# Latent attention: heads one at a time, the next pair's projections cut into pieces and set between the items, values multiplied so that the output comes out by feature

## The reference, cut to what matters

```python
q = jnp.einsum("bsc,chd->bshd", c_q, w_uq)              # 128 + 64 features for each head
q_nope, q_rope = q[..., :QK_NOPE], apply_rope(q[..., QK_NOPE:], cos, sin)
k_nope = jnp.einsum("bsc,chd->bshd", c_kv, w_uk)
v = jnp.einsum("bsc,chd->bshd", c_kv, w_uv)
s = (q_nope . k_nope + q_rope . k_rope) * scale         # causal mask, k_rope shared by the heads
p = softmax(s)
o = einsum("bhqk,bkhd->bqhd", p, v)
y = o.reshape(bsz, seq, N_HEADS * V_DIM) * silu(gate)
return y @ w_out
```

## Time and profile before

| what | value |
|---|---|
| median of three runs | 2797.47 us (2796.53 to 2798.96) |
| the profiled execution: time / span of its core | 2798.33 us / 2796.3 us |
| mean granted TensorE clock | 0.980 of full speed |
| busy over the span: PE, DVE, ACT, POOL | 2657.9, 1300.7, 719.2, 879.8 us |
| latent attention core, first projection to `wob` | 2320.0 to 2682.0 us |
| busy in it: PE, DVE, ACT | 322.6, 210.4, 85.1 of 362.0 us |

### The profile page before, as it was taken

One profiled execution on the slowest core, in us unless ns is written; L12 is line 12 of the kernel. 1 busy time (PEld: TensorE's weight loads), 2 busy tenths in 40 slices (PEclk: granted clock), 3 DMA queues, 4 the chain that ended last, 5 costly groups with the idle time before them and its releaser, 6 DMA issues. The chain is left out here.

```text
span 2796.3 us, 33364 instructions
## 1 busy us (share of the span) xinstructions
PE 2657.9 (95%) x13072; PEld 2194.7 (78%) x13072; DVE 1300.7 (47%) x1648; ACT 719.2 (26%) x941; POOL 879.8 (31%) x660
## 2 busy tenths in 40 slices
PE   6999999899899999999999999999998999898986
PEld 5888887677688888888888878788786778788875
DVE  4475533466453322123212464577845225555543
ACT  5144244222221200000000123455524122212221
POOL 3454423111233333333333443333343222110111
PEclk9999999999999999999999999999999999999998
DMA  3100121101341111111111112211133110000021
GB/s 125 46 31 31 42 72 38 53 35 46 147 143 46 49 49 47 51 45 53 45 53 46 68 53 83 87 45 45 45 127 112 42 56 29 19 10 15 23 83 68
DMA packets 44499, 160.72 MB, mean 57 GB/s; under 512 B 4720, under 2 KB 9072, under 8 KB 41968
## 3 DMA queue, kind: packets, MB, share of 16 engines
q1 hardware_dynamic: 38336, 124.53, 13.1%
q10 hardware_dynamic: 6064, 34.78, 3.3%
HBM read 138.33 MB, written 20.97 MB: 57 GB/s over the span
## 5 line engine op out<-in xcount | busy, mean ns | idle before, releaser
L428 POOL TENSOR_TENSOR derived_vectors<-w_staged 1x1 f32<-1x1 f32 x208 | 51.1, 246 | 1820.5 <-PE ps L544 1308.4
L431 POOL TENSOR_TENSOR w_low<-w_staged,w_high 128x1024 fp32r<-128x1024 f32 x208 | 557.3, 2679 | 16.7
L542 PE MATMUL ps<-h_ffn_high,w_high 128*128 128x512 f32 x832 | 324.6, 390 | 1.6 <-DVE ple_proj L1778 1.6
L544 PE MATMUL ps<-h_ffn_high,w_low 128*128 128x512 f32 x832 | 323.7, 389 | 0.0
L543 PE MATMUL ps<-h_ffn_low,w_high 128*128 128x512 f32 x832 | 323.7, 389 | 0.0
L607 PE MATMUL ps<-h_mix_high,w_high 128*128 128x512 f32 x688 | 281.9, 410 | 0.0
L609 PE MATMUL ps<-h_mix_high,w_low 128*128 128x512 f32 x688 | 269.2, 391 | 0.0
L608 PE MATMUL ps<-h_mix_low,w_high 128*128 128x512 f32 x688 | 268.1, 390 | 0.0
L429 POOL CAST w_high<-w_staged 128x1024 fp32r<-128x1024 f32 x208 | 215.0, 1034 | 0.0
L1760 DVE TENSOR_TENSOR squares<-ps,rstd 128x512 f32<-128x512 f32 x88 | 60.5, 689 | 322.1 <-PE ps L544 311.7
L542 PEld LDWEIGHTS ps<-h_ffn_high,w_high 128*128 128x128 f32 x832 | 156.2, 188 | 34.9 <-issue 2.5
(11 more groups left out here) (344 smaller groups left out, 5388.1 us busy)
## 6 DMA issues: line engine op xcount, KB each, us to landing
w_staged<-weights_in SPq DMA_DIRECT2D x200, 512.0 KB, 3.4
gates_loaded<-gates ACTq DMA_DIRECT2D x8, 1024.0 KB, 7.4
gates<-gates_staged_late SPq DMA_DIRECT2D x24, 256.0 KB, 2.0
x_in<-xT_in SPq DMA_DIRECT2D x4, 1024.0 KB, 9.5
x_mid<-xT_in ACTq DMA_DIRECT2D x1, 4096.0 KB, 12.8
x_spill_rnn<-x_mid ACTq DMA_DIRECT2D x8, 512.0 KB, 2.6
x_late<-x_spill_rnn ACTq DMA_DIRECT2D x4, 1024.0 KB, 7.8
x_spill_mla<-x_late ACTq DMA_DIRECT2D x1, 4096.0 KB, 11.1
```

What stands on the lines that cost most here:

```text
L428: nc.gpsimd.tensor_tensor(derived[0:1, 72:73], w_staged[0:1, j, 0:1], w_staged[0:1, j, 0:1], ALU.add)
L431: nc.gpsimd.tensor_tensor(w_low[:, j], w_staged[:, j], f32(w_high[:, j]), ALU.subtract).then_inc(s_split, 1)
L542: nc.tensor.matmul(ps[:, bank], wH, rhs[0][:, r, tok], start=(n == 0), stop=False)
L544: last = nc.tensor.matmul(ps[:, bank], wL, rhs[0][:, r, tok], start=False, stop=last_chunk)
```

## The change

`mla_projection(m)` numbers the projections as pieces, 16 to a pair, each one bank of results: 0 and 1 the rope queries by half, 2 and 4 the first head's other queries, 3 and 5 the rotations, 6 and 7 the first head's keys, 8 to 11 the values of both heads, 12 and 13 the second head's queries, 14 and 15 its keys. The items go head by head (`H` 0 to 7), `nk` 8 to 1 in each. Pieces 0 to 11 of the first pair run ahead of all items, in the banks 0 to 3; all later pieces run between the items as `MLA_FILLERS` places them: pieces 12 to 15 in items 1 to 4 of the even head, the next pair's pieces 0 to 11 in the odd head, two of them in items 1 to 4. All these go through bank 7, one at a time: a piece waits until DVE has read the one before (`s_pread`). An item with two pieces has one ahead of its scores and one behind.

The scaling moves: DVE takes the reciprocal (`mla_inverse`) as soon as the exponential is done, and ACT multiplies the probabilities with it ahead of the transposes (`mla_normed`, a copy with a scale, in place), for which the transposes now wait. The values product takes the values as the stationary operand, so that its result (bank 6) is by feature: `mla_out` and `mla_out_T` are gone, and `mla_gated` reads bank 6 directly. The values and the rotated rope queries have buffers of their own, two for the values. GpSimd's split waits for piece 13 where it would overwrite a unit still in use.

```diff
@@ -61,8 +61,20 @@
 for _name, _n, _T, _C in STREAM:
     STAGE[_name] = (_u, _t, _n, _T, _C)
     _u += _n
-    _t += _n * _T
+    _t += 0 if _name[:2] in ("uq", "uk") else _n * _T
 LOADS = _u
+
+
+MLA_COUNT = {0: 8, 1: 16, 2: 20, 4: 24, 6: 26, 7: 28, 8: 30, 9: 32, 10: 34, 11: 36, 12: 40, 13: 44, 14: 46, 15: 48}
+MLA_FILLERS = {0: ((), (12,), (13,), (14,), (15,), (), (), ()), 1: ((16,), (17, 18), (19, 20), (21, 22), (23, 24), (25,), (26,), (27,))}
+
+
+def mla_fillers(n):
+
+    H, r = n // 8, n % 8
+    return [16 * (H // 2) + i for i in MLA_FILLERS[H % 2][r]] if H < 7 else []
+
+
 K_UNIT = STAGE["uqr0"][0]
...
-        v_mla = at("v_mla", [P, NT, 2 * P], R(4, 8))
+        v_mla = [at(f"v_mla{k}", [P, NT, 2 * P], R(*place)) for k, place in enumerate(((4, 8), (2, 16)))]
+        rotated = at("q_rope_rotated", [P, S], R(4, 28))
...
-        mla = Attention("mla", [(2 * p + h, j, j + 1) for p in range(4) for j in reversed(range(NT)) for h in range(2)], P, SCALE_C, probs_c, probsT_c)
-
-        def mla_score_bank(n):
-
-            return 2 * ((n + STAGE[f"uqr{n // 16}"][1] + 1) % 2)
+        mla = Attention("mla", [(h, j, j + 1) for h in range(8) for j in reversed(range(NT))], P, SCALE_C, probs_c, probsT_c)
 
         def mla_scores_of(n):
-            b = mla_score_bank(n)
+            b = 2 * (n % 2)
             return ps[:, b:b + 2].rearrange("p b n -> p (b n)")[:, 0:mla.items[n][2] * P]
+
+        def mla_bank(m):
+            return m % 4 if m < 12 else 7
+
+        def mla_done(m):
+
+            return MM_PER_UNIT * (K_UNIT + 3 * (m // 16)) + MLA_COUNT[m % 16]
...
+            def mla_projection(m):
+
+                p, i = m // 16, m % 16
+                u0, bank = K_UNIT + 3 * p, mla_bank(m)
+                if m < 4:
+                    t = 6 + m // 2
+                    pe.wait_ge(s_free[m], use_of("cgate", 0, 6 + (bank_of("cgate", 0, 0) // 2 + m // 2) % 2) + 1)
+                elif m < 12:
+                    pe.wait_ge(s_pread, m - 3)
+                else:
+                    pe.wait_ge(s_pread, m)
+                if i in (0, 1):
...
+                elif i in (2, 4, 12, 13):
+                    t, h = (0, i // 2 - 1) if i < 12 else (1, i - 12)
+                    pe.wait_ge(s_split, u0 + 2)
+                    mla_matmuls(m, u0 + 1, 2 * P, 3, t * P, (cqH, cqL), h).then_inc(s_mm, 4)
+                elif i in (3, 5):
+                    h = i // 2 - 1
+                    pe.wait_ge(s_pread, 16 * p + h + 1)
+                    nc.tensor.matmul(ps[:, bank], rotate[:], q_rope[:, half_of(h)], start=True, stop=True).then_inc(s_rotq, 1)
+                elif i in (6, 7, 14, 15):
...
-                pe.wait_ge(mla.probed, n + 1)
+                pe.wait_ge(s_normed, n + 1)
...
+                await_at_least(pe, mla.outL, n)
                 for k in range(nk):
-                    last = nc.tensor.matmul(ps[:, 6 + n % 2, 0:P], mla.probsT[:, n % 2, k * P:(k + 1) * P],
-                                            v_mla[:, k, (h % 2) * P:(h % 2 + 1) * P], start=(k == 0), stop=(k == nk - 1))
+                    last = nc.tensor.matmul(ps[:, 6, 0:P], v_mla[H // 2 % 2][:, k, (H % 2) * P:(H % 2 + 1) * P],
+                                            mla.probsT[:, n % 2, k * P:(k + 1) * P], start=(k == 0), stop=(k == nk - 1))
                 last.then_inc(mla.summed, 1)
 
-            def mla_out_T(m):
-                pe.wait_ge(mla.out, m + 1)
-                nc.tensor.transpose(ps[:, 6 + m % 2, 0:P], o_mla[:, m % 2], ident[:]).then_inc(mla.outT, 1)
-
             pe.wait_ge(s_cwl, 5)
...
+            for m in range(12):
+                mla_projection(m)
+            pe.wait_ge(s_kr, 2)
+            mla_scores(0)
+            mla_scores(1)
+            for n in range(64):
+                fillers = mla_fillers(n)
+                mla_transposed(n)
+                if len(fillers) == 2:
+                    mla_projection(fillers[0])
+                if n + 2 < 64:
+                    mla_scores(n + 2)
+                if fillers:
+                    mla_projection(fillers[-1])
+                mla_values(n)
             pe.wait_ge(mla.outL, 64)
...
+            def mla_exp(n):
+                q, nk = n % 4, mla.items[n][2]
+                act.wait_ge(mla.negated, n + 1)
+                await_at_least(act, mla.transposed, n - 1)
+                nc.scalar.activation(mla.probs[:, n % 2, 0:nk * P], mla_scores_of(n), ACT.Exp,
+                                     bias=stat[:, 4 + q:5 + q], accum_out=stat[:, 8 + q:9 + q]).then_inc(mla.probed, 1)
+
+            def mla_normed(n):
+                q, nk = n % 4, mla.items[n][2]
+                act.wait_ge(mla.inverted, n + 1)
+                nc.scalar.activation(mla.probs[:, n % 2, 0:nk * P], mla.probs[:, n % 2, 0:nk * P], ACT.Copy,
+                                     scale=stat[:, 12 + q:13 + q]).then_inc(s_normed, 1)
+
+            for m in range(12):
+                if m == 6:
+                    mla_rope_high(0)
+                mla_high(m)
+            for n in range(2):
+                mla_exp(n)
+                mla_normed(n)
+            for n in range(64):
+                fillers = mla_fillers(n)
+                H, r = n // 8, n % 8
+                if H % 2 == 0 and r == 1:
+                    mla_rope_high(H + 1)
+                if H % 2 and H < 7 and r == 4:
+                    mla_rope_high(H + 1)
+                if len(fillers) == 2:
+                    mla_high(fillers[0])
+                if n + 2 < 64:
+                    mla_exp(n + 2)
+                if fillers:
+                    mla_high(fillers[-1])
+                if n + 2 < 64:
+                    mla_normed(n + 2)
...
+            def mla_inverse(n):
+                q = n % 4
+                dve.wait_ge(mla.probed, n + 1)
+                nc.vector.reciprocal(stat[:, 12 + q:13 + q], stat[:, 8 + q:9 + q]).then_inc(mla.inverted, 1)
...
+            def mla_gated(m):
+                H, j, _ = mla.items[m]
                 dve.wait_ge(mla.summed, m + 1)
+                y = cgate[:, H, j * P:(j + 1) * P]
+                nc.vector.tensor_tensor(y, ps[:, 6, 0:P], y, ALU.mult).then_inc(mla.outL, 1)
+
+            for m in range(12):
+                if m == 6:
+                    mla_rope_low(0)
+                mla_read(m)
+            dve.wait_ge(s_cg, DC)
+            for n in range(2):
+                mla_max(n)
+                mla_inverse(n)
+            for n in range(64):
+                fillers = mla_fillers(n)
+                H, r = n // 8, n % 8
+                if H % 2 == 0 and r == 1:
+                    mla_rope_low(H + 1)
+                if H % 2 and H < 7 and r == 4:
+                    mla_rope_low(H + 1)
+                mla_probs_copied(n)
+                if len(fillers) == 2:
+                    mla_read(fillers[0])
+                if n + 2 < 64:
+                    mla_max(n + 2)
+                if fillers:
+                    mla_read(fillers[-1])
+                mla_gated(n)
+                if n + 2 < 64:
+                    mla_inverse(n + 2)
...
```

More of the change, by code:

```diff
@@ L324, in fused_kernel @@
         s_rot, s_kr, s_cg = sem("k_rotated"), sem("k_rope_chain"), sem("mla_gate_silu")
-        s_rq, s_rotq, s_rqe, s_qready = [sem(f"q_rope_{n}") for n in ("raw", "rotated", "chain", "ready")]
+        s_rotq, s_rqe, s_qready = [sem(f"q_rope_{n}") for n in ("rotated", "chain", "ready")]
+        s_pread, s_normed = sem("mla_projection_read"), sem("mla_probs_normed")
         s_krH, s_krL, s_qrH, s_qrL = [sem(f"{n}_rope_{part}") for n in "kq" for part in ("high", "low")]
@@ L934, in mla_scores, with mla_matmuls @@
-            def mla_scores(n):
-                h, j, nk = mla.items[n]
-                p, hl = n // 16, h % 2
-                if n % 16 < 2:
-                    for t in range(2):
-                        pe.wait_ge(s_free[bank_of(f"ukv{p}", t, 1)], use_of(f"ukv{p}", 0, t) + 1)
-                    pe.wait_ge(s_qrL, 2 * p + 2)
+            def mla_matmuls(m, i_tile, pitch, chunks, column, high_low, h):
+                bank, slot = mla_bank(m), i_tile % 2
+                H, L = high_low
+                for c in range(chunks):
+                    wH = w_high[:, slot, c * pitch + column:c * pitch + column + P]
+                    wL = w_low[:, slot, c * pitch + column:c * pitch + column + P]
+                    nc.tensor.matmul(ps[:, bank], wH, H[:, c, half_of(h)], start=(c == 0), stop=False)
+                    nc.tensor.matmul(ps[:, bank], wH, L[:, c, half_of(h)], start=False, stop=False)
+                    last = nc.tensor.matmul(ps[:, bank], wL, H[:, c, half_of(h)], start=False, stop=(c == chunks - 1))
+                return last
@@ new lines, in mla_projection @@
+            def mla_projection(m):
[9 more added lines that the diff above has]
+                if i in (0, 1):
+                    pe.wait_ge(s_split, u0 + 1)
+                    mla_matmuls(m, u0, P, 3, 0, (cqH, cqL), i).then_inc(s_mm, 8)
```

(25 more changed lines are left out.)

227 lines of the change are left out of this document (62 added, 165 removed).

## The result

| | before | after |
|---|---|---|
| median | 2797.68 us (2796.53 to 2798.96, 4 runs) | 2759.13 us (2759.02 to 2760.46, 4 runs) |
| ratio | | 0.9863, 95% interval 0.9847 to 0.9878 |
| profiled execution: time / span | 2798.33 / 2796.3 us | 2760.46 / 2758.5 us |
| section, first piece to `wob` | 2319.99 to 2682.02: 362.0 us | 2321.30 to 2644.25: 323.0 us |

The kernel is 38.6 us faster; 37 were forecast. What comes ahead of it took 1.3 us longer there, and from `wob` on the two traces take the same 114.3 us.

A forecast was written before the change was run, and what follows sets the result against it. PE, with gaps, was taken to bound the section: 291 us work + 26.5 new waits + 4 clock + 3 output split = 325 against 362, so 37 saved and 2761 us forecast, range 2745 to 2779.

The forecast's parts named there:

- my 291 us of work: PE's work in the latent attention section once waits and output transposes are taken from 362.0 us; claimed unchanged by the change.
- the 325: Forecast length in us of the latent attention section after the change, against 362 before.
- The scaling on ACT: 64 scalings added to ACT, 1.05 down to 0.35 us each, 45 us in all, with no table load charged.
- Opening: Ahead of the first items: waits at the first rotation, banks, copies and first transposes, together 4.9 us.
- Even heads: Waits at small items, item of seven blocks and next head's first transposes: 2.0 us each, 8 in four heads.
- Odd heads: Pieces waiting for bank 7: 2.2 us at piece 24, 0.3, 0.4, 0.8 at 20, 22, 23; 10.4 in all.
- Last head: No fillers there; its last five items wait 2.4 us, about 3 with the end included.
- The clock: Falls of the granted clock in the section after waits: 4 us charged, where before 11 were lost.
- 26.5 of new waits: Section's new PE waits: opening 4.9, even heads 8, odd heads 10.4, last head 3, summed as 26 or 26.5 us.
- The single bank: Rival, chance 0.18: slower handoffs at the pieces' bank or more clock falls cut the saving; 2771 to 2783 us.
- Less wait than I walk: Rival, chance 0.10: short waits caught up, clock never falls; new waits near 12, section 306, time 2742 to 2751 us.
- Slower: Rival, chance 0.05: ring from exponential through scaling to transposes decides everywhere; at 0.5 us more per handoff, section 380, time 2816.

The follow-up runs named there:

- the by-feature part alone: Kernel before with scaling moved to ACT ahead of the transposes and values as stationary operand, projections still between the pairs: 2763.97 us.
- the experiment with bank 5: Changed kernel with value pieces 8 and 10 of the later pairs in bank 5 instead of bank 7: 2752.61 us.
- a whole second pass: Changed kernel with ACT writing each item's scaled probabilities twice, first into a buffer that nothing reads: 2777.89 us.
- two such moves: Changed kernel with the rope split one item later in odd heads, 2758.50 us; changed kernel with piece 4 ahead of piece 3 in the opening, 2760.08 us.
- the version with the later rotation: Changed kernel with the first rotation (piece 3) behind query piece 4 in the opening: 2760.08 us.

## Why the prediction was right, point by point

- **The work of PE, and where luck comes in.** The section is 323.0 us. Less 3.0 for the split and 1.7 for the clock, 318 are left; with my 291 us of work the waits would be 27. Counted from the issue (each start against the usual distance behind a matmul of that form), the trace has 29 stands of more than 0.15 us, 23.0 in all: 4.5 in the opening, 7.5 in the even heads, 9.1 in the odd heads and 1.9 in the last one. So I had the waits 3.5 too high and the work some 4 too low, and the two cancel in the 325. That the change leaves the work as it is was not quite right either. The same count gives 292 for the kernel before, without its output transposes, and 295 here: the first matmul of a piece takes 0.28 us behind scores (from 2393.63 to 2393.91), not 0.23. The values product of eight blocks still takes 1.83 to 1.84 us from start to start, with the operands exchanged: that term was right at nothing.

```profile
2621.90 2.00 PE L1004 MATMUL ps<-probs_mla_T,v_mla 128*128 128x128 f32 x16
2623.74 0.93 PE L994 MATMUL ps<-identity,probs_mla 128*128 128x128 f32 x7
```

- **The scaling on ACT.** I took 1.05 to 0.35 us a pass, 45 in all; it is 49.7:

```profile
L1400 ACT ACTIVATE probs_mla<-probs_mla,softmax_stats 128x1024 f32<-128x1024 f32 (+3 forms) x64 | 49.7, 777 | 58.0 <-DVE softmax_stats L1979 58.0
...
L1394 ACT ACT_TABLE_LOAD x1 | 1.3, 1283 | 0.0
```

  One table load, though exponential and copy alternate 64 times. The rule of the Trainium skill (ScalarE: Activation LUTs, "Table sets: the hidden batching unit") is about functions of different sets; these two need no change of table here. The one load took 1.28 us, and no run has a switch between two sets.
- **Opening.** 4.9 forecast. The waits are 1.34 at the rotation, 0.83 ahead of the scores and 1.87 ahead of the first transposes: 4.0, and 4.6 from the issue.
- **Even heads.** 2.0 each forecast, 1.9 from the issue. The small items have 0.29 and 0.27 (0.5 and 0.4 from the issue, where 0.5 each was walked), the next head's first transposes 0.48 (0.65), and item 1 has 0.29 from the issue.
- **Odd heads.** 2.2 ahead of piece 24 was forecast, 2.15, 2.09 and 2.13 came. Piece 23 waits 0.5 (0.7 from the issue, 0.8 walked). The 0.3 and 0.4 at pieces 20 and 22 did not come: in head 1 both start 0.06 to 0.07 us behind the last score matmul, at 2400.07 and 2405.89. The four waits walked also add to 3.7 a head, not to the 3.5 of my sum.
- **Last head.** The last items wait 0.56 and 0.47, all four stands 1.9 from the issue; 3 us were walked for the whole head.
- **The clock** is the term that was off in the saving: 4 us charged, 1.7 measured. That is most of the 2 us by which the section came out below 325. Ahead of the split of the outputs it fell once, behind the 2.15 us at piece 24 in head 1, and neither behind the like wait in heads 3 and 5 nor in the opening.
- **Why 39 and not more.** My sum subtracts 29 us of waits ahead of the values product and 12.6 ahead of the value projections, and puts 26.5 of new waits against them. The experiments show what that hides: the by-feature part alone has 35.0 us of the 38.6, and the pieces bring most of what they bring a second time. On top of it they take away the 12.3 us of stands, 2.3 of the 6.1 us of waits for the scaling ahead of transposes, and some 5 us of low clock (four falls against one). They give most of it back at bank 7, at the rotation and first scores of the opening, ahead of the values product of small items and in the 0.05 us of each piece. What is left is 5.0 us by the sections.
- **Rivals.** The single bank bit no harder than walked: three waits of 2.1, worth 6.5 us with their fall of the clock by the experiment with bank 5. "Less wait than I walk" needed 12 us; the list alone has 17. "Slower" needed 1.7 us more of scaling for each item; a whole second pass, 0.78 on average, cost 18.8. The 380 us of that rival do not follow from its own terms: 0.5 more on six handoffs over two items, less 0.5 of slack, is 1.0 for each of 64 items, which on 325 makes 389.

## What to carry to other kernels

A wait in the order of one engine can be removed in two ways, by taking links out of the ring or by putting independent work into the gap, and the second is worth little once the first is done (here 35.0 us for one, 38.6 for both): price them together, and try each alone before writing both. Independent work that goes through one PSUM bank needs, between its pieces, as much other work as the bank takes to be emptied, here 1.4 us behind the modelled end for a high and a low part; one bank borrowed for the two worst pieces gave 6.5 us. When a pass is moved to the next item to free one wait, look at what it then stands in front of; two such moves here changed nothing.

## What the hardware showed unexpectedly

- A scaling copy on ACT by a factor for each partition takes 1.149 us for 1024 columns from SBUF to SBUF; the plain copy of the same size in the earlier trace rows takes 1.045. I had taken the two as equal. The plain copy also writes fp32r, not f32; which of the two differences makes the 0.1 us no run shows.

```profile
L1400 ACT ACTIVATE probs_mla<-probs_mla,softmax_stats 128x1024 f32<-128x1024 f32 x8 | 9.2, 1149 | 1.8 <-DVE softmax_stats L1979 1.8
```

- Waits of about the same length are followed by a fall of the granted clock or not: the 2.15 us at piece 24 in head 1 was, the 2.09 and 2.13 of heads 3 and 5 were not. The 1.9 us ahead of the first transposes was not, while in the version with the later rotation, with the same wait (1.85), the mean granted clock of the 4 us from 2348.8 on was 0.57. In the kernel before the clock stood at 0.50 from 2494.7 to 2498.1, though from the issue no stand since 2431 had been longer than 0.91 us. The fall in head 1 lasted 3.4 us, which is 1.7 by the granted clock. By starts it cost about 1.6: from piece 24 to the transposes behind its values product, head 1 takes 3.96 us (2414.04 to 2418.00), head 3 takes 2.41 (2494.00 to 2496.41).
